# Cached keys of a decode step turned by VectorE instead of TensorE, with the cache loaded in strips of 32 partitions

## What is computed

```python
def dilated_attention_sample(q, k_all, v_all, rel_bias):     # (128,1), (512,4), (2048,16)
    q_idx = L - T + jnp.arange(T)
    for (w, d) in DILATED_PATTERNS:
        dist = d * jnp.arange(w // d + 1)
        idxs.append(q_idx[:, None] - dist[None, :]); biases.append(pattern_bias(rel_bias, d, w // d))
    ...
    s = jnp.einsum('bthc,btkhc->bthk', q, k_all[:, idx]) * (HEAD_DIM ** -0.5) + bias
    p = jax.nn.softmax(s, axis=-1)
    return jnp.einsum('bthk,btkhc->bthc', p, v_all[:, idx])
```

```python
    u = gc * hc
    u_ext = jnp.concatenate([u_prev, u], axis=1)
    conv = conv_w[0] * u_ext[:, 0:T] + conv_w[1] * u_ext[:, 1:1 + T] + conv_w[2] * u_ext[:, 2:2 + T]
    y_conv = gb * conv
```

## Time and profile before

| | us |
|---|---|
| three runs | 1078.85, 1081.19, 1085.17 (median 1081.19) |
| profiled execution | 1082.67, of which the span is 1080.7 |
| PE busy over the span | 1036.0 (96%) |
| DVE, ACT, POOL busy | 523.0 (48%), 312.7 (29%), 212.4 (20%) |
| convolution stage, first to last product | 280.06 to 498.08 |
| of it the 128 and 96 transposes of keys, busy on PE | 19.2 and 15.7 |
| of it their copies on ACT | 19.1 and 15.5 |

### The profile page before, as it was taken

One profiled execution on the slowest core, in us unless ns is written; L12 is line 12 of the kernel. 1 busy time (PEld: TensorE's weight loads), 2 busy tenths in 40 slices (PEclk: granted clock), 3 DMA queues, 4 the chain that ended last, 5 costly groups with the idle time before them and its releaser, 6 DMA issues.

```text
span 1080.7 us, 15684 instructions
## 1 busy us (share of the span) xinstructions
PE 1036.0 (96%) x5834; PEld 620.1 (57%) x5834; DVE 523.0 (48%) x1175; ACT 312.7 (29%) x665; POOL 212.4 (20%) x240
## 2 busy tenths in 40 slices
PE   7999999999999999999999999989999999889997
PEld 6888875565878777766555554334433333345443
DVE  6836634777733464545556464441111110047674
ACT  2332313777533322301111123111111111244331
POOL 0100001121433352531012111322231110130000
PEclk9999999999999999999999998989999999989999
DMA  9713214940563666663973237989999999974321
GB/s 315 190 31 116 71 50 119 293 101 6 215 213 112 212 211 216 207 244 81 355 270 128 94 105 280 405 340 414 418 410 410 419 420 399 371 288 157 119 78 78
DMA packets 99260, 242.11 MB, mean 224 GB/s; under 512 B 21206, under 2 KB 56958, under 8 KB 84528
## 3 DMA queue, kind: packets, MB, share of 16 engines
q1 hardware_dynamic: 88544, 212.10, 54.1%
q0 software_dynamic: 9920, 26.38, 6.4%
q10 hardware_dynamic: 720, 2.62, 0.6%
HBM read 210.12 MB, written 35.65 MB: 227 GB/s over the span
## 4 chain that ended last, share of the span: by engine, by line
PE 80%; DVE 6%; DMA 6%; SPq 4%; issue 2%; ACT 2%; POOL 0%; POOLq 0%; DVEq 0%; ACTq 0%
PE pair L2921 13%; PE pair L3124 13%; PE pair L2598 10%; PE pair L2976 9%; PE pair L3146 6%; PE pair L3228 5%; PE pair L3223 3%; PE pair L2739 2%; DMA h_dram<-R 2%; DMA R<-in_w_up 2%; PE pair L2713 2%; PE pair L3047 2%; PE pair L2755 2%; PE pair L3111 1%; SPq L707 1%
## 5 line engine op out<-in xcount | busy, mean ns | idle before, releaser
L2921 PE MATMUL pair<-R 128*128 128x264 f32 x672 | 160.2, 389 | 0.2 <-POOL R L1032 0.2
L3124 PE MATMUL pair<-R 128*32 128x512 f32 (+2 forms) x896 | 151.3, 601 | 5.2 <-DMA R<-in_w_up 3.0
L2598 PE MATMUL pair<-R 128*128 128x256 f32 x672 | 149.7, 382 | 0.4 <-DVE R L1755 0.4
L2598 PEld LDWEIGHTS pair<-R 128*128 128x128 f32 x672 | 127.0, 191 | 18.8 <-issue 1.0
L2921 PEld LDWEIGHTS pair<-R 128*128 128x128 f32 x672 | 123.5, 190 | 23.4 <-issue 3.5
L2976 PE MATMUL pair<-R 128*128 128x512 f32 x256 | 116.6, 606 | 0.0
L2329 DVE TENSOR_TENSOR R<-pair,R 128x256 f32<-128x256 f32 x21 | 8.9, 425 | 208.3 <-ACT R L1516 208.3
L3124 PEld LDWEIGHTS pair<-R 128*32 128x32 f32 (+2 forms) x896 | 48.8, 125 | 92.2 <-issue 87.8
L3146 PE MATMUL pair<-R,bias 128*32 128x512 f32 (+2 forms) x448 | 78.0, 611 | 2.7 <-issue 2.1
L2976 PEld LDWEIGHTS pair<-R 128*128 128x128 f32 x256 | 47.7, 192 | 53.3 <-issue 52.6
L3228 PE MATMUL pair<-R 128*128 128x512 f32 x168 | 73.0, 593 | 0.0
(11 more groups left out here) (366 smaller groups left out, 1471.5 us busy)
## 6 DMA issues: line engine op xcount, KB each, us to landing
R<-in_w_gate SPq DMA_DIRECT2D x32, 1024.0 KB, 12.3
R<-in_w_up SPq DMA_DIRECT2D x32, 1024.0 KB, 15.6
R<-in_w_down SPq DMA_DIRECT2D x32, 1024.0 KB, 16.8
R<-in_w_in SPq DMA_DIRECT2D x12, 1024.0 KB, 8.4
R<-in_x_prompt SPq DMA_DIRECT2D x16, 512.0 KB, 3.8
R<-in_cache_k SPq DMA_DIRECT2D x8, 1024.0 KB, 5.0
R<-in_cache_v SPq DMA_DIRECT2D x8, 1024.0 KB, 4.9
R<-y_dram SPq DMA_DIRECT2D x16, 512.0 KB, 5.9
```

Of the source, the lines that this page charges most:

```text
L2598: last = mm(qbank(p, part, k), lhs[:, c, :], rhs[:, c, :], start=(c == 0), stop=(c == 3))
L2921: last = mm(cbank(n, k), lhs[:, c, :], rhs[:, c, :], start=(c == 0), stop=(c == 3))
L3124: last = mm(bk[2 + u][r, :].rearrange("p (w f) -> p w f", w=2), xgT[u][:, c, r], wgu[s][:, :, c, :], start=(c == 0), stop=(c == DC - 1))
```

## The change

* **Keys.** A quarter of a key item is turned by two DVE transposes of 32x32 squares, 512 and 384 elements a partition, from KV straight into one buffer `kT`, which is single: the first quarter of the next sequence waits until PE's `score` of this one is done. PE's transposes and ACT's copies are gone. A partition strip of 32 now holds a quarter of the rows, so queries are laid out by strip (`spread_q` on DVE, one for each sequence) and `score` becomes 16 products of 256 columns in place of 12 of 512, 384 and 32.
* **Softmax by pairs of sequences.** `soft`, `norm` and `turn` run four times, for two sequences each; minimum and sum are joined over four groups of rows with small DVE transposes and reductions (`by_group`). `turn` is four plain products with a permuted identity, which ACT copies in six instructions.
* **Loads.** Far keys come in four DMAs of 32 partitions, near values in four and far values in four (five DMAs for a key item, eight for a value item; four each before). A key buffer is free when DVE has turned it.
* **Order.** On DVE a slot's tap comes ahead of its sample part. The items' order and the parts' slots are new (below).
* **Earlier stages.** The eight small DMAs of the position bias (128 elements each, 512 before) move on SP behind two stores of x; DVE copies them out. The bias of the sample part is added in five DVE instructions, three before. The new tokens' q and k are turned in 32 products, eight transposes before; 16 DVE copies (`q4`, 128 elements on 32 partitions) are added to steps 9 to 24 of the prompt attention.

The core of the diff:

```diff
+    kT = view(R1, 15392, 16, ROW)
+            if kind == "k":
+                sp.dma_start(kv[:, 0:4, :].rearrange("p c d -> p (c d)"),
+                             ck[b][PAST - NEAR:PAST, :].rearrange("(p c) d -> p (c d)", c=4)).then_inc(arrived, 16)
+                far_rows = ck[b][0:far_at, :].rearrange("(k r a) d -> a r k d", k=FARC, a=16)
+                for i in (0, 2, 1, 3):
+                    sp.dma_start(kv[strips[i], 4:7, :], far_rows[i]).then_inc(arrived, 16)
+                return
+            near_rows = cv[b][PAST - NEAR:PAST, :].rearrange("(i r c) d -> c r i d", c=4, i=4)
+            for c in (0, 2, 1, 3):
+                sp.dma_start(kv[strips[c], 0:4, :], near_rows[c]).then_inc(arrived, 16)
...
+        def turn_keys(b, gg):
+            slot, arrived = item("k", b)
+            kv = KV[slot]
+            if gg == 0:
+                dve.wait_ge(S(f"ring_in{slot}"), arrived)
+                if b >= 1:
+                    dve.wait_ge(S("ss_done"), b)
+                else:
+                    dve.wait_ge(S("ssa_full"), 1)
+            raw = kv[:, :, P * gg:P * gg + P].rearrange("p c (n x) -> p c n x", n=4)
+            out = kT[:, 4 * gg:4 * gg + 4, 0:PART].rearrange("p n (c r) -> p c n r", c=7)
+            dve.transpose(out[:, 0:4], raw[:, 0:4])
+            dve.transpose(out[:, 4:7], raw[:, 4:7]).then_inc(S("kt_done"), 1)
+        def by_group(cols, op, src, group, out):
+            then(dve.transpose(cols, src))
+            then(dve.tensor_reduce(group, cols.rearrange("p (h i t) -> p h t i", h=2, i=4), AX.X, op))
+            if op == ALU.add:
+                then(dve.reciprocal(group, group))
+            return dve.transpose(out.rearrange("p (h i t) -> p h i t", h=2, i=4),
+                                 group.rearrange("p (h t) -> p h t", h=2).unsqueeze(2).broadcast_to([P, 2, 4, NT]))
         def score_sample(g):
+            dve.wait_ge(S("ss_done"), 2 * g + 2)
+            for s in range(2):
+                then(dve.tensor_tensor_reduce(Es[:, s, :], bk[6 + g % 2][:, ROW * s:ROW * s + ROW], bias_s, -1.0, 3e38, ALU.add, ALU.min,
+                                              least[:, s:s + 1]))
+                if 2 * g + s + 1 < NB:
+                    new_bias(2 * g + s + 1)
+            by_group(least_t, ALU.min, least, group_least, nms).then_inc(S("ss_scored"), 1)
+            for b in (2 * g + 2, 2 * g + 3):
+                if b < NB:
+                    spread_q(b)
         def normalise_sample(g):
+            dve.wait_ge(S("ss_exp"), 2 * g + 2)
+            then(by_group(dens_t, ALU.add, dens, group_den, rdens))
+            for s in range(2):
+                dve.tensor_scalar(Es[:, s, :], Es[:, s, :], rdens[:, s:s + 1], None, ALU.mult).then_inc(S("ps_ready"), 1)
...
+                if n >= 1 and k < 3:
+                    taps(n - 1, k)
                 for part in PARTS_AT.get(at, ()):
                     sample_part(*part)
-                if n >= 1 and k < 3:
-                    taps(n - 1, k)
...
-        def keys(b, gg):
-            for r in range(4):
-                last = pe.transpose(bk[4][:, P * r:P * r + P], kv[:, r, P * gg:P * gg + P], ident[:, :])
-            for k in range(FARC):
-                last = pe.transpose(bk[5][:, P * k:P * k + P], kv[:, 4 + k, P * gg:P * gg + P], ident[:, :])
         def score_keys(b):
+            pe.wait_ge(S("kt_done"), NG * b + NG)
+            for hh in range(2):
+                for half in range(2):
+                    for j in range(NG):
+                        n = 4 * j + 2 * hh + half
+                        at = 32 * n + (0 if hh else 16)
+                        last = mm(out[strips[j], ROW * second:ROW * second + ROW], qbd_all[second][:, at:at + 32], kT[:, n, :], ...)
         def turn_ps(g):
+            pe.wait_ge(S("ps_ready"), 2 * g + 2)
+            for c in range(4):
+                last = mm(bk[4][:, P * c:P * c + P], Es[:, c // 2, P * (c % 2):P * (c % 2) + P], by_quarter, start=True, stop=True)
```

More of the change, by code:

```diff
@@ L197 @@
[L197 to L206, removed]
@@ L207, with sample_order @@
-ROOM = {"key": 4, "score": 4, "turn": 6, "weigh": 8, "sum": 4}
+    return i % 3, sum(ARRIVES[k] for k, _ in ITEMS[i % 3:i + 1:3])
+RING_USED = tuple(sum(ARRIVES[k] for k, _ in ITEMS[s::3]) for s in range(3))
+def sample_order():
+    parts = []
+    for g in range(NPASS + 1):
+        keys = [[("key", 2 * g + d, gg) for gg in range(NG)] if g < NPASS else [] for d in range(2)]
+        if g == 0:
+            parts += keys[0] + [("score", 0)] + keys[1] + [("score", 1), ("soft", 0)]
+            continue
+        b = 2 * g - 2
+        parts += [*keys[0][0:1], ("norm", g - 1), *keys[0][1:2], ("turn", g - 1), *keys[0][2:4]]
+        if g < NPASS:
+            parts += [("score", 2 * g)]
+        parts += [("weigh", b), *keys[1][0:2], ("sum", b), ("weigh", b + 1), *keys[1][2:4]]
+        if g < NPASS:
+            parts += [("score", 2 * g + 1), ("soft", g)]
+        parts += [("sum", b + 1)]
+    return parts
@@ L210 @@
+SAMPLE_PARTS = sample_order()
+ROOM = {"key": 4, "score": 6, "soft": 2, "norm": 2, "turn": 4, "weigh": 8, "sum": 4}
 CONV_PAIRS = (("u", 0), ("u", 1), ("y", 0), ("u", 2), ("u", 3), ("y", 2))
@@ L224, with place_of @@
 PARTS_AT = spread_parts()
-def place_of(kind, b, gg=None):
-    return next(s for s, parts in PARTS_AT.items() for part in parts if part[0:2] == (kind, b) and (gg is None or part[2] == gg))
+def place_of(part):
+    return next(s for s, parts in PARTS_AT.items() if part in parts)
 NSTAT = 6
@@ L2096, in sample_part @@
         def sample_part(kind, b, *more):
-            if "norm" in more:
-                normalise_sample(0 if kind == "key" else 1)
+            if kind == "key":
+                turn_keys(b, more[0])
+            if kind == "soft":
+                score_sample(b)
+            if kind == "norm":
+                normalise_sample(b)
             if kind == "weigh":
                 mask_sample(b)
-            if "soft" in more:
-                score_sample(b // 4)
-            if kind == "score" and b == 3:
-                spread_q(1)
-                new_bias(1)
             if kind == "sum":
                 keep_sum(b)
-            if "sum" in more:
-                keep_sum(more[-1])
         dve.wait_ge(S("late_in"), 16 * NLATE)
@@ L2888, in sample_part @@
         def sample_part(kind, *more):
-            if kind == "key":
-                keys(more[0], more[1])
             if kind == "score":
@@ L2896, in sample_part @@
                 weigh_values(more[0])
-            if kind == "sum" or "sum" in more:
-                sum_values(more[-1])
+            if kind == "sum":
+                sum_values(more[0])
         def conv_product(n, k):
```

313 lines of the change are left out of this document (147 added, 166 removed).

## The result

The changed kernel takes 1104.22 us (1100.37 to 1109.48), the kernel before 1083.18 (1078.85 to 1085.24): a ratio of 1.0203, interval 1.0145 to 1.0261. Slower by 21 us, outside the stated range and on the other side. The profiled execution has a span of 1100.5 us against 1080.7, 19.8 more.

A forecast was written before the change was run, and what follows sets the result against it. PE's list was taken to bound the convolution stage: -22.1 + 17.7 (waits for DVE) + 1.2 (weights) + 0.8 - 0.5 (other stages) = -2.9 us, giving 1078.3 us; range 1060 to 1094.

The forecast's parts named there:

- PE's list: Convolution stage: key parts removed, `score` and `turn` longer, old 0.9 us wait gone; -22.1 us.
- The price of a key part: DVE's transposes of one key part in the convolution stage: 1.06 us, from sums over as many elements.
- The two ends, 0.72 and 1.54: Range for DVE's key part: 0.72 us at a one-source instruction's rate, 1.54 us if stretched beside POOL.
- A: Convolution stage: cheap transposes, 0.72 us a key part, give 1071 us, with better overlapping waits 1060; chance 0.24.
- B: Convolution stage: DVE becomes the bound; at 1.54 us a key part chains are 10 us longer, 1088 us; chance 0.17.
- PE's waits for DVE: Convolution stage: `score` and `turn` wait for DVE's work one slot earlier; 17.7 us in eleven waits.
- the list: PE's and DVE's instructions in the convolution stage laid side by side by slot, giving each `score` and `turn` wait.
- The weights' chain: Convolution stage: blocks' weights issued behind items on SP; block 7 waits 0.8, block 10 0.6; +1.2 us without old waits.
- rival C: Loads into 32-partition strips run slower and delay blocks' weights; at half rate +10.5 us, 1089 us; chance 0.13.
- Other stages: Outside the convolution stage: new tokens' q and k +0.8, `q4` copies hidden at 0, position bias -0.5 us.
- the forecast's own mechanism: Convolution stage: PE's list shrinks, but waits for DVE and weights take most of it back; 1078.3 us; chance 0.46.

The follow-up runs named there:

- b4_early_t: Changed kernel with the four DVE subtractions (`conv_t`) for the convolution's second half moved to other slots; 1102.19 us, ratio 1.0158 to the kernel before.
- a2_weights: Changed kernel with the loads of blocks' weights moved earlier in SP's order; 1098.34 us, ratio 1.0148 to the kernel before.
- b1_spread: Changed kernel with `score` in quarters two slots behind DVE, each quarter's products going to four strips in turn; 1101.94 us, ratio 1.0184 to the kernel before.
- b3_both: Changed kernel with the edits of `b1_spread` and `a2_weights` together; 1086.01 us, ratio 1.0016 to the kernel before.
- a1_split: Changed kernel with `score` in quarters two slots behind DVE, each quarter's products writing one strip; 1122.59 us, ratio 1.0366 to the kernel before.

## Why the prediction was wrong, point by point

The mechanism was named: the stage lasts as long as PE's list with the waits for DVE and the weights. The step that failed is the sum of these waits, with what follows them. The prediction had 17.7 us of waits for DVE, 1.2 for weights and full clock behind both; the trace shows 25.9, 6.8 and 8.0 us of half clock.

* **PE's list** (-22.1 with the old wait): right in kind, 2.1 us too hopeful. `turn` takes 1.00, not 0.87 (0.5 for four); `score` takes 1.86 for the 1.88 worked out. The other 1.6 us are not traced.
* **The price of a key part** (1.06, from sums of as many elements): right. The transposes take 0.62 and 0.46 from start to start,

```profile
L2111 DVE STREAM_TRANSPOSE R<-R 128x512 f32<-128x512 f32 x32 | 22.4, 700 | 0.3 <-PE pair L2884 0.3
L2112 DVE STREAM_TRANSPOSE R<-R 128x384 f32<-128x384 f32 x32 | 17.0, 533 | 0.0
```

  1.08 us a part. Though POOL is busy for 83.69 us of the stage they show no stretch: the 32 long ones lie between 0.66 and 0.71. The two ends, 0.72 and 1.54, and with them rivals A and B in the form in which they were put, fall. (The 0.72 doesn't follow from its row either: 0.49 for 528 elements makes 0.83 for 896.) For what the Trainium skill states of one-input instructions (SBUF — State Buffer, Who interferes with whom) the trace agrees.
* **PE's waits for DVE** (17.7, measured 25.9): right in most places, wrong in three. Eight of the twelve places came within 0.8 us of the list (score 2 1.40 for 1.3, score 3 0.88 for 1.05, score 5 1.06 for 1.0, turn 2 1.62 for 1.7, turn 3 3.17 for 3.0, turn 0 3.28 for 2.5, score 7 and turn 1 none for 0.3 and 0), and `score` 0 with the new wait ahead of it makes 3.36 for 3.0. Three did not. `score` 4 waited 5.34 for 1.7: the list left out `conv_t`, as `b4_early_t` shows for 2.35 us of it. `score` 1 waited 2.69 for 1.05 and `score` 6 3.09 for 1.1: there POOL sums a block's weights at the same time, and DVE's sums with both operands in SBUF take twice as long as in the list, as here ahead of `score` 1 (a line of DVE's timeline, then one of POOL's):

```profile
308.25 1.79 DVE L1983 TENSOR_TENSOR R<-R 128x264 f32<-128x264 f32 x2 [2.91 <-ACT R L1401]
...
308.15 0.73 POOL L1061 TENSOR_TENSOR R<-R 128x256 f32<-128x256 f32 x1 [15.81 <-DMA R<-in_w_in]
```

  1.71 us from the start of the two joins to the next instruction, where the list had 0.9. In `a2_weights` the same sums of POOL begin only when these two joins are nearly done, and the joins take 0.82:

```profile
308.39 0.90 DVE L1984 TENSOR_TENSOR R<-R 128x264 f32<-128x264 f32 x2 [2.90 <-ACT R L1402]
...
309.00 0.88 POOL L1062 TENSOR_TENSOR R<-R 128x256 f32<-128x256 f32 x1 [16.52 <-DMA R<-in_w_in]
```

  `score` 1 waits for 1.79 us there, 0.90 less, which is what the two joins save. The row with the mean of 0.619 was in view and was used for the upper end of a transpose, where it doesn't belong, and not for the joins, where it does. For `score` 6 POOL's part is read from the overlap alone.
* **The weights' chain** (+1.2): mis-sized, 6.8. The prediction gave blocks 7 and 10 0.8 and 0.6; they waited 2.23 and 2.22, and blocks 4 and 5 1.87 and 0.50 besides. The issues of an item ahead of the weights it had; the later landing it had under rival C alone, whose 2.5 us for keys nearly came (2.4 and 1.8) and whose 5 us for values did not (0.9 and 1.5). By the rule of the Trainium skill that it weighed there (SBUF — State Buffer, Door 1: The DMA port swizzle) transfers into 32 partitions should be slower. The four landings agree in direction; that it is the strips and not the number of DMAs no run here shows.
* **The clock**: no step of the prediction had it. It forecast 18.9 us of standing still in a stage that had known 1.1, and let PE run at full clock behind each wait. 8.0 us; in the sum the second largest error after the waits for DVE (8.2), ahead of the weights (5.4), PE's list (2.1) and the other stages (-1.0). Together they are the 22.7 us between -2.9 and +19.8.
* **Other stages**: not contradicted. The copies in the prompt attention are hidden (93.42 us against 93.06); the rest (+0.3 foretold, -0.7 measured) is less than the stages behind scatter by.
* **The rivals**: the forecast's own mechanism decided: its signs came, but larger than it had them (16.0 us behind the transposes for 8 to 12, 8.1 behind the division for 5 to 8), and beside them C's sign, waits for the weights, with 5.4 us over the list where C had 10.5. Each rival was a change of one price. What was missing is a rival that adds up small lateness of several kinds. `b1_spread` and `b3_both` show why: waits hide one another, so a wait that is worked out as absent (weights) comes forward as soon as another is taken.

## What to carry to other kernels

When work moves from a full engine to one with slack, the shorter list is worth what the distance between producer and consumer lets through: with one slot of distance the 19.1 us came back as waits and half clock, with three slots, the same work in quarters and the weights ahead in the queue, 11 us stayed in the stage. Price each wait with the clock that may follow it, and list every instruction of the producer's slots, those that the change doesn't touch too, at the durations they have beside the other engines. When a wait is removed, look in the list of waits for the one that it hid, before judging the edit by its time.

## What the runs showed of the hardware that was not expected

* Products into different strips of 32 output partitions run beside each other, products into one strip behind each other: four f32 products of 256 columns take 1.84 us into one strip (`a1_split`) and 0.57 into four (`b1_spread`); sixteen into four strips 1.86. The Trainium skill has the first half of this (TensorE: Matmul & The Clock Gate, Part 3: Packing small matmuls — row/col tiling: matmuls at different tile positions of the array run concurrently), and the runs agree. The loop over strips has to be the inner one.
* In a stage that is otherwise full, waits of PE between 1.9 and 8 us were in 39 of 52 cases followed by a stretch of 3.4 to 6.8 us at half clock, so that `score` 4 with its 5.34 us of waiting cost 1.7 us more behind it, and the product after it 0.4.
